# Reordering the decay scan of a two-block model on all engines: level by level instead of unit by unit

## The chip, the cores and the metric

The kernel runs on one core of one Trainium2 chip, in float32. The metric is the device time of one execution in microseconds (us), the median of several runs. The engines are PE (matrix products, with PEld for its weight loads), DVE, ACT, POOL (elementwise work) and SP (starts transfers). Each has its own queue of instructions, worked off in order, and waits on semaphores of the others.

## What is computed

The reference is two transformer blocks of two layers each, 512 tokens by 1024 features. The second block's layers have a mixer of three parts, of which the third is a recurrence with a decay for each key dimension, run forward and backward over the tokens and added (6 heads, keys and values of 64, chunks of 64 tokens; `bt` is the running sum of the log decays):

```
def step(state, inp):
    qt, kt, vt, bt = inp
    diff = bt[:, :, :, None, :] - bt[:, :, None, :, :]
    decay = jnp.where(lower, jnp.exp(jnp.where(lower, diff, 0.0)), 0.0)
    scores = jnp.einsum('bhtk,bhsk,bhtsk->bhts', qt, kt, decay)
    o = (jnp.einsum('bhts,bhsv->bhtv', scores, vt)
         + jnp.einsum('bhtk,bhkv->bhtv', qt * jnp.exp(bt), state))
...
o_r = o_f + o_b
o_r = o_r * lax.rsqrt(jnp.mean(o_r * o_r, axis=-1, keepdims=True) + EPS)
rec = (o_r * jax.nn.silu(g_rec.astype(f32))).astype(h.dtype)
mixed = jnp.concatenate([a, att, rec], axis=-1)
return mixed @ w_out.astype(h.dtype)
```

## The kernel before

The program is a list of phases that every engine walks through. Most of PE's time is in the dense products (line 1320). Each of the two layers of the second block has one phase of kind "scan". It stands between the layer's attention and the rest of the product with `w_out`, and it is all that the change touches.

**Blocks and units.** The six heads lie in three blocks of two (128 partitions). Each block is done in two directions, so a scan has six units, u = 0 to 5: block b = u // 2, direction d = u % 2 (0 forward, 1 backward). Even units are forward, odd ones backward. `blk` and `v` count blocks and levels through both scans.

**A unit's score matrix** of 512 x 512 for each head is built from two kinds of products:
- Pairs. For tiles of 128 tokens that differ, the decay is split at a tile's end: `end_decays` (ACT, exponentials of the sums from `E`) makes factors in `KF` and `QF`, `weigh_ends` (DVE, lines 2580 and 2581, 128x512) multiplies them with keys and queries, `end_queries` (ACT, line 1837) scales three tiles more into `QX`. PE multiplies (line 1215): 20 matmuls in 8 groups forward (the diagonal tiles for both directions are among them, with `KS`, the sum of both directions' keys from POOL, line 2931), 12 in 6 groups backward. Each group goes to one of two PSUM banks, and ACT copies it into `AM` (line 1860).
- Levels. Within the diagonal tiles the decay is split at the middle of sub-blocks of 7 sizes (`LEVELS`: 64, 32, 1, 2, 4, 8, 16). `level_exponents` (DVE, lines 2569 and 2570, 14 instructions of 128x256) makes the differences in `WL`, `level_decays` (ACT, line 1847, one instruction of 128x3584) their exponentials. `weigh_levels` (DVE, line 2592, 7 instructions) multiplies the key half with the keys. `queries` (POOL, line 2910, 28 instructions of 64x128 a unit) multiplies the query half with the queries, into one of eight buffers that lie in spare columns of `X` and `H` (resid and hbuf in the rows). PE multiplies (line 1230, 4 matmuls a level) into one of two PSUM banks. ACT copies the first two levels into `AM` (line 1878), DVE the other five with predicated copies (`merge`, line 2611, two a level).

When both directions of a block are in `AM`, PE multiplies with the values (line 1245, 8 matmuls of 128x512). ACT squares the result (line 1887), PE sums it (`sum_rec`, line 1296), DVE adds epsilon (`begin_finish`, lines 2618 and 2622), POOL takes the root (line 2921), PE spreads it (`spread_rec`, line 1305) and DVE multiplies (`finish`, line 2627).

**Early parts.** The product with `w_out` has 8 output groups. Five eighths of each, whose input is ready before the scan ends, are computed inside the scan: `early` (line 1277, five matmuls of 128x512 for a group from the third on), two PSUM banks in turn; `keep_early` (ACT, line 1899) copies the bank out with a scale, `add_early` (POOL, line 2943) adds it to the residual. `EARLY_AT` says at which unit each group stands.

**Order before.** On PE a unit is: pairs, one early group, 7 levels, and in odd units the values. DVE does, for each unit, the exponents of the next unit, its ends, the five merges of this unit, and the seven weighings of the next. ACT: pair copies, `keep_early`, two level copies, exponentials of the next unit. POOL: all queries of a unit, then an early add, every second time a root. Semaphores tie them: PE's level v waits for `query_ready` (v + 1), for `level_weighed` once a unit, and for `level_taken` (v - 1), which frees the bank.

## Time and profile before

| | us |
|---|---|
| runs | 3520.06, 3520.62, 3513.16 |
| median | 3520.06 |
| the profiled execution | 3523.34 |
| its span | 3521.0 |
| PE busy | 3322.7 (94%) |
| DVE busy | 2146.7 (61%) |
| POOL busy | 1582.4 (45%) |
| ACT busy | 972.7 (28%) |

The rows of the trace are those of the one profiled execution. Its mean granted TensorE clock is 0.969 of 2.4 GHz. The first scan lies from 2073 to 2239 us, the second from 2918 to 3081. A float32 matmul shows as two records, so a level of four matmuls is x8. DVE and ACT start an instruction before the one ahead has ended, so that the distance from start to start is shorter than the duration of one.

### The profile page before, as it was taken

To read this page: it belongs to the slowest core of one execution; us is meant where nothing else is said; L and a number is where in the kernel's file an instruction comes from. 1 tells how busy PE (TensorE), PEld (TensorE's weight loads), DVE (VectorE), ACT (ScalarE), POOL (GpSimd) and SP (SyncE) were. 2 spreads that over 40 slices of the span, in tenths; PEclk is the share of its full clock that TensorE was granted. 3 is DMA by queue.
4 is the path that set the end of the run, shared out by engine and by line. 5 is a ranking of instruction groups with operands and counts; after the bars stand their busy time and mean duration, and the time that the engine had idled before them with its cause. 6 is when DMAs were issued, how large, how long until landed. Compare 5 with 4: busy or idle time off the path is not lost.

```text
span 3521.0 us, 44753 instructions
## 1 busy us (share of the span) xinstructions
PE 3322.7 (94%) x16056; PEld 2551.9 (72%) x16056; DVE 2146.7 (61%) x3556; ACT 972.7 (28%) x2203; POOL 1582.4 (45%) x1534
## 2 busy tenths in 40 slices
PE   8979999999999999999999978899999978899998
PEld 5656555555557967888888746688888865678887
DVE  7577756544544296555646668488764777645554
ACT  2066211001121174211122264322212345332211
POOL 1044322222235224444454458466544547645554
PEclk9999999999999999999999988999999998999999
DMA  7300223333312200344422100244443200022232
GB/s 252 131 3 2 102 79 131 108 114 120 102 56 73 83 1 31 121 161 161 162 91 88 63 12 9 79 145 153 164 142 97 89 28 16 10 88 84 90 90 78
DMA packets 91097, 317.68 MB, mean 90 GB/s; under 512 B 10816, under 2 KB 13152, under 8 KB 90880
## 3 DMA queue, kind: packets, MB, share of 16 engines
q1 hardware_dynamic: 64224, 218.34, 18.9%
q10 hardware_dynamic: 24768, 90.19, 6.9%
q0 software_dynamic: 1888, 6.29, 0.7%
q8 instruction: 132, 2.16, 0.2%
q14 instruction: 85, 0.70, 0.1%
HBM read 312.68 MB, written 2.10 MB: 89 GB/s over the span
## 4 chain that ended last, share of the span: by engine, by line
PE 85%; DVE 9%; ACT 3%; issue 2%; POOL 1%; DMA 0%; DVEq 0%; ACTq 0%; SPq 0%; POOLq 0%
PE ps L1320 64%; PE ps L1322 4%; PE ps L629 3%; PE ps L1277 1%; PE ps L1230 1%; PE ps L985 1%; PE ps L999 1%; PE ps L1021 1%; PE ps L1173 1%; PE ps L1057 1%; PE ps L1215 1%; DVE arena L2611 1%; DVE hbuf L2238 1%; DVE arena L2569 1%; ACT arena L1499 1%
## 5 line engine op out<-in xcount | busy, mean ns | idle before, releaser
L1320 PE MATMUL ps<-arena 128*128 128x256 f32 (+1 forms) x3744 | 951.4, 408 | 4.0 <-DVE arena L2264 3.9
L1320 PEld LDWEIGHTS ps<-arena 128*128 128x128 f32 x3744 | 710.8, 190 | 208.8 <-issue 5.6
L2740 POOL TENSOR_TENSOR arena<-ring,arena 128x512 f32<-128x512 f32 (+1 forms) x140 | 182.6, 1304 | 843.7 <-PE ps L1320 843.7
L1320 PE MATMUL ps<-arena,ring 128*128 128x256 f32 (+1 forms) x2032 | 524.9, 410 | 3.1 <-ACT arena L1668 3.1
L1320 PE MATMUL ps<-hbuf,ring 128*128 128x256 f32 (+1 forms) x1824 | 475.1, 415 | 14.9 <-ACT hbuf L1775 13.4
L1320 PEld LDWEIGHTS ps<-arena,ring 128*128 128x128 f32 x2032 | 385.3, 190 | 119.5 <-ACT arena L1668 5.9
L1320 PEld LDWEIGHTS ps<-hbuf,ring 128*128 128x128 f32 x1824 | 358.3, 197 | 113.7 <-issue 19.1
L2285 DVE TENSOR_TENSOR arena<-ps,arena 128x256 f32<-128x256 f32 (+1 forms) x192 | 86.1, 449 | 362.1 <-PE ps L1320 236.6
L2172 DVE CUSTOM_DVE_ANT_0 aring<-aring,csil,adab 128x1024 f32<-128x1024 f32 x176 | 261.2, 1505 | 1.7
L2290 DVE SCALAR_TENSOR_TENSOR resid<-ps,mod,resid 128x256 f32<-128x256 f32 (+2 forms) x296 | 137.4, 482 | 189.7 <-PE ps L1320 185.1
L2723 POOL TENSOR_TENSOR arena<-ring 128x512 f32<-128x512 f32 (+1 forms) x140 | 179.9, 1285 | 157.2 <-PE ps L1320 149.2
L2290 DVE SCALAR_TENSOR_TENSOR resid<-arena,mod,resid 128x256 f32<-128x256 f32 (+1 forms) x168 | 108.3, 664 | 207.6 <-ACT arena L1668 204.3
L1668 ACT ACTIVATE arena<-ps 128x256 f32<-128x256 f32 (+1 forms) x152 | 62.9, 414 | 610.1 <-PE ps L1320 580.8
L2734 POOL TENSOR_TENSOR arena<-ring 128x512 f32<-128x512 f32 (+1 forms) x140 | 220.8, 1577 | 0.0
L2810 POOL TENSOR_SCALAR arena<-arena,small 128x512 f32<-128x512 f32 (+2 forms) x144 | 98.7, 697 | 239.7 <-DVE small L2053 239.7
L2729 POOL TENSOR_TENSOR arena<-arena,ring 128x512 f32<-128x512 f32 (+1 forms) x140 | 190.4, 1360 | 18.6
L1659 ACT ACTIVATE arena<-ps 128x256 f32<-128x256 f32 (+1 forms) x168 | 68.0, 405 | 469.3 <-PE ps L1320 459.0
L1320 PE MATMUL ps<-hbuf,arena 128*128 128x256 f32 (+1 forms) x672 | 175.8, 404 | 0.0
L2740 POOL TENSOR_TENSOR csil<-ring,junk 128x512 f32<-128x512 f32 x40 | 52.0, 1301 | 227.4 <-PE ps L1320 168.6
L1320 PEld LDWEIGHTS ps<-hbuf,arena 128*128 128x128 f32 x672 | 127.7, 190 | 34.4
L1632 ACT ACTIVATE rstd<-ps 128x256 f32<-128x256 f32 (+1 forms) x180 | 73.6, 409 | 267.9 <-PE ps L1320 250.6
L2379 DVE SCALAR_TENSOR_TENSOR arena<-arena 128x512 f32<-128x512 f32 x88 | 141.8, 1611 | 3.1
(321 smaller groups left out, 5365.5 us busy)
## 6 DMA issues: line engine op xcount, KB each, us to landing
aring<-in_ada ACTq DMA_DIRECT2D x172, 512.0 KB, 4.7
ring<-in_mlp SPq DMA_DIRECT2D x128, 512.0 KB, 3.7
ring<-in_up SPq DMA_DIRECT2D x88, 512.0 KB, 3.3
ring<-in_in SPq DMA_DIRECT2D x56, 512.0 KB, 3.2
ring<-in_down SPq DMA_DIRECT2D x32, 512.0 KB, 3.5
ring<-in_odd_in SPq DMA_DIRECT2D x24, 512.0 KB, 3.2
arena<-in_ada SPq DMA_DIRECT2D x16, 512.0 KB, 13.8
ring<-in_out SPq DMA_DIRECT2D x16, 512.0 KB, 3.2
```

The source lines that it names most:

```text
L629: mm = nc.tensor.matmul(slot[:, lo:hi], ring[:, c % RING, k, :], src[:, kt, lo:hi], start=kt == k0, stop=kt == k0 + nkt - 1)
L1320: return nc.tensor.matmul(ps[:, bank, 0:p.tw], w, x, start=start, stop=stop, skip_group_check=True)
L1322: mm = nc.tensor.matmul(ps[:, bank, t * P:(t + 1) * P], x[:, t * P:(t + 1) * P], w, start=start and t == 0, stop=stop, skip_group_check=True)
L2172: nc.vector.tensor_tensor_reduce(wt, wt, csil[:, 0, :], 1.0, adab[:, layer, nb:nb + 1], ALU.mult, ALU.add, mod[:, layer, nb, 0:1]).then_in ...
L2285: return nc.vector.tensor_tensor(home(p, half, lo, lo + tw), turned_view(p, product), turned_view(p, kept), ALU.add)
L2290: x = nc.vector.scalar_tensor_tensor(out=X[:, blk, a_:b_], in0=src[:, a_ - lo:b_ - lo], scalar=mod[:, layer, p.gate + blk, s_:s_ + 1], in1 ...
L2379: nc.vector.scalar_tensor_tensor(out=v, in0=u[:, 2:S + 2], scalar=CFW[:, blk, 2:3], in1=v, op0=ALU.mult, op1=ALU.add).then_inc(conv_out, 1)
L2723: nc.gpsimd.tensor_tensor(s[0], f1[:, 0:h], f1[:, h:2 * h], ALU.add).then_inc(wsum_ready, 1)
L2729: nc.gpsimd.tensor_tensor(s[1], s[0], f0[:, 0:h], ALU.subtract).then_inc(wsum_ready, 1)
L2734: nc.gpsimd.tensor_tensor(s[2], f0[:, 0:h], f1[:, 0:h], ALU.subtract).then_inc(wsum_ready, 1)
L2740: nc.gpsimd.tensor_tensor(s[3], f0[:, h:2 * h], s[1], ALU.subtract).then_inc(wsum_ready, 1)
L2810: nc.gpsimd.tensor_scalar(v, v, small[:, 12 + i % 4:13 + i % 4], 1.0, ALU.mult, ALU.mult).then_inc(pair_scaled, 1)
```

## The change

The scan is written in another order on every engine. No instruction of the levels and pairs on PE, and none of the exponents, ends, merges and exponentials, is added or dropped.

- DVE: the exponents of unit 1 come before the levels of unit 0, and the ends are weighed two units ahead. Inside a unit each level is weighed and its query made in one go (`weigh_level`, one instruction of 128x256 and two of 64x256), and merges follow two levels behind. The queries have moved here from POOL, where they were 28 instructions a unit.
- PE: the pairs of an odd unit are computed between the levels of the even unit ahead of it, one group behind each level from the second on. The pairs of an even unit follow the values. Early groups 3 to 7 belong to units 0 to 4 and are cut into five single matmuls, one behind each level from the third on; groups 0 to 2 stay ahead of the first pairs. `sum_rec` is ahead of the even units' levels, `spread_rec` behind the second level of the odd units. Each level now waits for its own `level_weighed`.
- ACT: copies one pair group or one level at a time, in PE's order. The exponential of the next unit stands behind the pair copies in even units. At the start it makes the end decays of units 0 and 1 and empties the first early bank before it waits for DVE.
- POOL: keeps the sums of keys, the early adds, the roots and the clearing of the spare columns. Its waits for its own queries are gone.
- The values wait for `so_taken` (the second step of the norm) instead of `syt_taken` (the last).
- In the query buffers each head's part is contiguous, and PE reads its 128 columns as two runs of 64.

```diff
         EARLY_BANK = (5, 7, 5, 7, 5, 7, 5, 7)
-        EARLY_AT = {(0, "ends"): range(0, 3), **{(u, "levels"): range(2 + u, 3 + u) for u in range(1, 6)}}
+        EARLY_FIRST, EARLY_OF = 3, {u: 3 + u for u in range(5)}
         LATE_GROUPS, LATE_K = (0, 1), 2
...
 
             def scan(i):
                 n = scan_phases.index(i)
-                for b in range(3):
+
+                def pair_group(u, hx, j):
+                    b, d = u // 2, u % 2
                     blk = 3 * n + b
...
+                    rows = slice(64 * hx, 64 * hx + 64)
...
+                    pe.wait_ge(unit_ready, 2 * blk + d + 1)
...
+                    if r >= 2:
+
+                        pe.wait_ge(pair_taken, r - 1)
+                    for t in (range(j, 4) if d == 0 else range(j)):
...
+                        mm = nc.tensor.matmul(ps[:, r % 2, t * P:(t + 1) * P], lhs, rhs, start=True, stop=True)
+                    mm.then_inc(pair_ready, 1)
+
+                def level(u, li):
+                    d = u % 2
+                    v = 42 * n + 7 * u + li
...
+                    pe.wait_ge(query_ready, v + 1)
+                    pe.wait_ge(level_weighed, v + 1)
+                    if v % 42 == 0:
+
+                        pe.wait_ge(spare_cleared, 2 * (n + 1))
+                    if v >= 2:
+
+                        pe.wait_ge(level_taken, v - 1)
+                    for t in range(4):
...
+                    mm.then_inc(level_ready, 1)
+
+                def values(b):
+                    blk = 3 * n + b
+
+                    pe.wait_ge(level_taken, 14 * blk + 14)
+                    pe.wait_ge(pair_taken, pair_index(blk, 1, 1, 3) + 1)
+                    if blk >= 1:
+
+                        pe.wait_ge(so_taken, blk)
...
-                        early(i, EARLY_AT.get((2 * b + d, "levels"), ()))
-                        if d == 0 and b >= 1:
-                            sum_rec(blk - 1)
-                        for li in range(7):
...
+                    mm.then_inc(so_ready, 1)
+
+                early(i, range(EARLY_FIRST))
+                for hx in range(2):
+                    for j in range(4):
+                        pair_group(0, hx, j)
+                for u in range(6):
+                    b, d = u // 2, u % 2
+                    if d == 0 and b >= 1:
+                        sum_rec(3 * n + b - 1)
+                    for li in range(7):
+                        level(u, li)
+                        if d == 0 and li >= 1:
+                            pair_group(u + 1, (li - 1) // 3, 1 + (li - 1) % 3)
+                        if li >= 2 and u in EARLY_OF:
+                            k = li - 2
+                            early_part(i, EARLY_OF[u], range(k, k + 1), k == 0, k == EARLY - 1)
+                        if d == 1 and b >= 1 and li == 1:
+                            spread_rec(3 * n + b - 1)
+                    if d == 1:
+                        values(b)
+                        if u < 5:
                             for hx in range(2):
-                                mm = nc.tensor.matmul(ps[64 * hx:64 * hx + 64, SO_BANK, :], VR[:, j, P * b + 64 * hx:P * b + 64 * hx + 64],
-                                                      AM[:, hx, j, :], start=j == 0, stop=j == 3)
-                        mm.then_inc(so_ready, 1)
+                                for j in range(4):
+                                    pair_group(u + 1, hx, j)
                 begin_late(i, LATE_GROUPS[0])
                 sum_rec(3 * n + 2)
                 begin_late(i, LATE_GROUPS[1])
...
                 nc.scalar.activation(roots[:, 0, KT - 1:KT], small[:, 40:41], ACT.Exp)
                 end_decays(0)
+                end_decays(1)
+                keep_early(range(0, 1))
                 end_queries(0)
-                keep_early(EARLY_AT[0, "ends"][0:1])
-                end_decays(1)
-                keep_early(EARLY_AT[0, "ends"][1:2])
                 level_decays(0)
-                keep_early(EARLY_AT[0, "ends"][2:])
+                keep_early(range(1, 2))
+                for hx in range(2):
+                    for j in range(4):
+                        take_pair(0, hx, j)
+                        if (hx, j) == (0, 1):
+                            keep_early(range(2, 3))
+                end_queries(1)
                 for u in range(6):
                     blk, d = 3 * n + u // 2, u % 2
-                    take_pairs(u)
-                    keep_early(EARLY_AT.get((u, "levels"), ()))
-                    take_levels(u)
+                    take_level(u, 0)
+                    take_level(u, 1)
+                    if d == 0:
+                        take_pair(u + 1, 0, 1)
+                        take_pair(u + 1, 0, 2)
+                    end_decays(u + 2)
+                    if d == 0:
+                        take_pair(u + 1, 0, 3)
+                        for j in range(1, 4):
+                            take_pair(u + 1, 1, j)
                     level_decays(u + 1)
-                    end_queries(u + 1)
-                    end_decays(u + 2)
+                    if u in EARLY_OF:
+                        keep_early(range(EARLY_OF[u], EARLY_OF[u] + 1))
+                    end_queries(u + 2)
                     if d == 1:
                         square_values(blk)
+                        if u < 5:
+                            for hx in range(2):
+                                for j in range(4):
+                                    take_pair(u + 1, hx, j)
...
-                def weigh_levels(u):
-                    if u >= 6:
-                        return
+                def weigh_level(u, li):
...
                     dve.wait_ge(level_decay, 6 * n + u + 1)
-                    for li, m in enumerate(LEVELS):
-                        w = WL[:, 7 * (1 - d) + li, :].rearrange("p (g x m) -> p x g m", x=2, m=m)[:, d]
-                        k = KR[:, 3 * d + b, :].rearrange("p (g x m) -> p x g m", x=2, m=m)[:, d]
-                        x = nc.vector.tensor_tensor(w, w, k, ALU.mult)
-                    x.then_inc(level_weighed, 1)
...
+                    both = WL[:, 7 * (1 - d) + li, :].rearrange("p (g x m) -> p x g m", x=2, m=m)
+                    k = KR[:, 3 * d + b, :].rearrange("p (g x m) -> p x g m", x=2, m=m)[:, d]
+                    nc.vector.tensor_tensor(both[:, d], both[:, d], k, ALU.mult).then_inc(level_weighed, 1)
...
+                    if v >= 8:
+
+                        dve.wait_ge(level_ready, v - 7)
+                    w = both[:, 1 - d].rearrange("p (a g) m -> p a g m", a=2)
+                    q = QR[:, b, :].rearrange("p (a g x m) -> p x a g m", a=2, x=2, m=m)[:, 1 - d]
+                    to = level_queries(v).rearrange("p a (h g m) -> p h a g m", h=2, m=m)
+                    for hx in range(2):
+                        rows = slice(64 * hx, 64 * hx + 64)
+                        x = nc.vector.tensor_tensor(to[rows, hx], w[rows], q[rows], ALU.mult)
+                    x.then_inc(query_ready, 1)
+
+                def merge(u, li):
...
+                    dve.wait_ge(pair_taken, pair_index(blk, 0, 1, 3) + 1)
+
+                    dve.wait_ge(level_ready, v + 1)
+
+                    dve.wait_ge(level_taken, v)
...
+                weigh_ends(0)
                 level_exponents(0)
-                weigh_ends(0)
-                weigh_levels(0)
+                weigh_ends(1)
                 for u in range(6):
                     blk, d = 3 * n + u // 2, u % 2
                     level_exponents(u + 1)
-                    weigh_ends(u + 1)
+                    for li in range(7):
+                        weigh_level(u, li)
+                        if li >= 3:
+                            merge(u, li - 1)
+                    merge(u, 6)
+                    if d == 0 and u > 1:
+                        begin_finish(blk - 1)
                     if d == 1 and u > 1:
                         finish(blk - 1)
-                    if d == 0 and u > 1:
-                        begin_finish(blk - 1)
-                    merge(blk, d)
-                    weigh_levels(u + 1)
+                    weigh_ends(u + 2)
                 begin_finish(3 * n + 2)
                 finish(3 * n + 2)
...
-                    def queries(u):
-
...
-                        pool.wait_ge(level_decay, 6 * n + u + 1)
...
-                                rows = slice(64 * hx, 64 * hx + 64)
-                                for half in range(2):
-                                    x = nc.gpsimd.tensor_tensor(dst[rows, half, hx], w[rows, 2 * half:2 * half + 2],
-                                                                q[rows, 2 * half:2 * half + 2], ALU.mult)
-                            x.then_inc(query_ready, 1)
...
-                    def both_keys(b, level):
+                    def both_keys(b):
                         blk = 3 * n + b
-                        if level:
-
-                            pool.wait_ge(query_ready, level)
+                        if b:
+
                             pool.wait_ge(pair_ready, pair_index(blk - 1, 0, 1, 3) + 1)
...
+                    both_keys(0)
+                    def add_early(share):
...
                     for u in range(6):
-                        if u and u % 2 == 0:
-                            both_keys(u // 2, 42 * n + 7 * u)
-                        queries(u)
-                        add_early(EARLY_AT.get((u, "levels"), ()), 42 * n + 7 * u + 7)
+                        if u in (0, 2):
+                            both_keys(u // 2 + 1)
+                        if u in EARLY_OF:
+                            add_early(range(EARLY_OF[u], EARLY_OF[u] + 1))
                         if u >= 2 and u % 2 == 0:
-                            roots(3 * n + u // 2 - 1, 42 * n + 7 * u + 7)
-                    roots(3 * n + 2, 42 * n + 42)
+                            roots(3 * n + u // 2 - 1)
+                    roots(3 * n + 2)
```

PE, first scan, units 0 and 1. Lines 1215, 1230, 1277 and 1245 are pairs, levels, early parts and values. Before:

```order
968 L1215 MATMUL ps<-arena 128x128 x20
969 L1230 MATMUL ps<-resid,arena 128x128 x16
970 L1230 MATMUL ps<-hbuf,arena 128x128 x12
971 L1215 MATMUL ps<-arena 128x128 x12
972 L1277 MATMUL ps<-hbuf,ring 128x512 x5
973 L1230 MATMUL ps<-hbuf,arena 128x128 x4
974 L1230 MATMUL ps<-resid,arena 128x128 x16
975 L1230 MATMUL ps<-hbuf,arena 128x128 x8
976 L1245 MATMUL ps<-arena 64x512 x8
```

After the change, to the middle of unit 0 (lines 1214, 1230 and 1301 are pairs, levels and early parts):

```order
968 L1214 MATMUL ps<-arena 128x128 x20
969 L1230 MATMUL ps<-resid,arena 128x128 x8
970 L1214 MATMUL ps<-arena 128x128
971 L1230 MATMUL ps<-resid,arena 128x128 x4
972 L1214 MATMUL ps<-arena 128x128 x2
973 L1301 MATMUL ps<-hbuf,ring 128x512
974 L1230 MATMUL ps<-resid,arena 128x128 x4
975 L1214 MATMUL ps<-arena 128x128 x3
976 L1301 MATMUL ps<-hbuf,ring 128x512
977 L1230 MATMUL ps<-hbuf,arena 128x128 x4
978 L1214 MATMUL ps<-arena 128x128
979 L1301 MATMUL ps<-hbuf,ring 128x512
```

The 12 pair matmuls of unit 1 and the early group that stood between the two units are now between the levels of unit 0.

DVE, first scan, from the last merges of unit 0 to the first weighings of unit 1. Before, the merges of unit 0 (line 2611) are followed by the weighings of unit 1 (line 2592) at once:

```order
1943 L2611 COPY_PREDICATED arena<-arena,ps 128x4x8x8 x2
1944 L2611 COPY_PREDICATED arena<-arena,ps 128x4x4x16 x2
1945 L2592 TENSOR_TENSOR arena<-arena 128x4x64
1946 L2592 TENSOR_TENSOR arena<-arena 128x8x32
1947 L2592 TENSOR_TENSOR arena<-arena 128x256
1948 L2592 TENSOR_TENSOR arena<-arena 128x128x2
```

After the change (2658 merge, 2618 and 2619 ends, 2607 and 2608 exponents of unit 2; the weighing and the query of a level, 2629 and 2639, come behind the 14 exponents):

```order
1950 L2658 COPY_PREDICATED arena<-arena,ps 128x4x8x8 x2
1951 L2658 COPY_PREDICATED arena<-arena,ps 128x4x4x16 x2
1952 L2618 TENSOR_TENSOR arena<-arena 128x512
1953 L2619 TENSOR_TENSOR arena<-arena 128x512
1954 L2607 TENSOR_TENSOR arena<-aring 128x4x64
1955 L2608 TENSOR_TENSOR arena<-aring 128x4x64
1956 L2607 TENSOR_TENSOR arena<-aring 128x8x32
```

Between the last merge of a unit and the first query of the next there now stand the two instructions on the ends and the 14 exponents of the unit after next.

## Rows read from the trace of the kernel before

**Rows 1.** The page: the chain that ended last, by engine.
```profile
PE 85%; DVE 9%; ACT 3%; issue 2%; POOL 1%; DMA 0%; DVEq 0%; ACTq 0%; SPq 0%; POOLq 0%
```

**Rows 2.** By stretch: length; busy PE, PEld, DVE, ACT, POOL; granted clock; DMA share, GB/s.
```profile
2073.30:2238.70 165.40, 137.94 (x732) 96.45 (x732) 110.79 (x207) 74.76 (x160) 117.08 (x186) 0.89 0.04 13
2917.80:3081.40 163.60, 140.33 (x733) 98.62 (x733) 114.71 (x207) 74.76 (x160) 114.22 (x186) 0.89 0.04 14
2131.00:2136.00 5.00, 4.29 (x24) 4.13 (x24) 3.46 (x8) 3.06 (x11) 4.65 (x9) 0.71 0.02 3
2179.40:2185.70 6.30, 5.46 (x24) 5.20 (x24) 3.59 (x9) 2.43 (x9) 5.89 (x13) 0.54 0.01 4
...
2140.00:2154.00 14.00, 13.85 (x60) 9.38 (x60) 11.15 (x18) 4.64 (x10) 8.99 (x16) 0.76 0.00 0
2189.00:2205.00 16.00, 15.83 (x84) 11.09 (x82) 10.32 (x20) 6.15 (x16) 8.87 (x13) 0.89 0.05 12
2982.00:2996.00 14.00, 13.83 (x56) 8.68 (x54) 10.97 (x19) 4.14 (x10) 8.00 (x14) 0.76 0.00 0
3032.00:3043.00 11.00, 10.83 (x60) 7.62 (x58) 9.86 (x18) 4.52 (x10) 5.96 (x11) 1.00 0.00 0
```

**Rows 3.** PE in order of time, first scan: start, us, line, count, idle before.
```profile
2085.18 6.71 PE L1277 MATMUL ps<-hbuf,ring 128*128 128x512 f32 x10 [4.71 <-ACT junk L1899]
...
2118.06 4.56 PE L1277 MATMUL ps<-hbuf,ring 128*128 128x512 f32 x10
...
2131.06 2.04 PE L1230 MATMUL ps<-resid,arena 128*128 128x128 f32 x8 [4.24 <-DVE arena L2611]
...
2136.20 3.65 PE L1245 MATMUL ps<-arena 128*64 128x512 f32 x16 [0.85 <-DVE arena L2611]
...
2153.80 2.03 PE L1230 MATMUL ps<-hbuf,arena 128*128 128x128 f32 x16
...
2162.95 1.89 PE L1215 MATMUL ps<-arena 64*128 64x128 f32 x14
...
2189.34 5.91 PE L1215 MATMUL ps<-arena 64*128 64x128 f32 x40
...
2202.08 3.09 PE L1230 MATMUL ps<-hbuf,arena 128*128 128x128 f32 x24
...
2210.21 1.09 PE L1305 MATMUL ps<-ident,small 128*64 128x128 f32 x16
...
2228.26 3.65 PE L1245 MATMUL ps<-arena 128*64 128x512 f32 x16 [0.85 <-DVE arena L2611]
...
2238.76 7.13 PE L629 MATMUL ps<-hbuf,ring 128*128 128x512 f32 x16 [0.84 <-DVEq L578]
```

**Rows 4.** DVE in order of time, first scan, columns as in Rows 3.
```profile
2082.76 0.68 DVE L2581 TENSOR_TENSOR arena<-arena 128x512 f32<-128x512 f32 x1
2090.69 2.44 DVE L2592 TENSOR_TENSOR arena<-arena 128x256 f32<-128x256 f32 x7 [7.25 <-ACT arena L1847]
2093.05 0.42 DVE L2569 TENSOR_TENSOR arena<-aring 128x256 f32<-128x256 f32 x1
...
2097.95 1.55 DVE L2580 TENSOR_TENSOR arena<-arena 128x512 f32<-128x512 f32 x1
...
2110.76 0.77 DVE L2611 COPY_PREDICATED arena<-arena,ps 128x256 f32<-128x256 int32 x2 [0.57 <-PE ps L1230]
...
2119.19 0.73 DVE L2569 TENSOR_TENSOR arena<-aring 128x256 f32<-128x256 f32 x1
...
2150.53 0.74 DVE L2618 SCALAR_TENSOR_TENSOR hbuf<-ps,arena 128x512 f32<-128x512 f32 x1
```

**Rows 5.** POOL in the first scan, grouped: one of its two groups of queries.
```profile
L2910 POOL TENSOR_TENSOR resid<-arena 64x128 f32<-64x128 f32 x88 | 48.8, 572 | 6.2 <-issue 3.3
```

**Rows 6.** POOL in order of time, first scan: an early add.
```profile
2092.76 6.19 POOL L2943 TENSOR_TENSOR resid<-resid,junk 128x512 f32<-128x512 f32 x1 [3.77 <-ACT junk L1899]
```

**Rows 7.** ACT in order of time, first scan: the exponential of one unit.
```profile
2106.74 3.19 ACT L1847 ACTIVATE arena<-arena 128x3584 f32<-128x3584 f32 x1
```

153 lines of the change are left out of this document (56 added, 97 removed).

## The prediction

> **What bounds the kernel now.** I read the page first. The chain of work that ended last is 85% PE [rows 1], so time is gained only where PE stands still or runs at the low clock. The change touches only the two scans. The table by stretches gives them: 165.4 and 163.6 us, in which PE is busy 137.9 and 140.3 us, DVE 111 and 115, POOL 117 and 114, and the granted clock is 0.89 in both [rows 2]. So each scan holds about 25 us of PE standing still, and low clock for (1 - 0.89) / 0.5 = 22% of 165 us, 36 us (0.5 is the level of 1.2 GHz, 1.0 that of 2.4). That is the room.
>
> Next the order of time on PE. The reader is to see one wait, 4.24 us for a DVE copy, inside the second unit of a block [rows 3]: DVE works through 14 exponent instructions before it copies level products out. Nothing like it is in the first unit of a block. The DVE rows say why it is slow: the same 128x256 instruction takes 0.42 us at one place and 0.73 at another [rows 4]. POOL is at its 64x128 query instructions at the second place. At the first it has one add under way, which takes 6.19 us, as long as DVE's whole row of instructions [rows 6]. The two hold each other up.
>
> **Names.** A unit u is one direction of one block of two heads; d = u % 2. A scan has units 0 to 5. E is the time at which PE can start level 0 of an even unit. All terms are at the full clock first.
>
> **What the change removes and adds.** POOL loses its query instructions, 168 a scan (28 a unit), 572 ns each in the larger group [rows 5]. DVE gets 14 query instructions a unit, each 64 partitions by 256 elements. The trace has none. The nearest row is its own weighing of 256 elements, 7 in 2.44 us, 0.335 each [rows 4]; the far end is 0.65, for the 0.73 that such an instruction takes beside POOL (0.42 is 0.335 from start to start) [rows 4]. I take 0.335, since POOL's work beside it falls to 14 instructions a scan (three key sums, eight adds, three roots). Weighing and query of one level are then 3 x 0.335 = 1.0 us, a merge (two predicated copies) 0.77 [rows 4].
>
> PE's work is the same. Per level 0.98 us (24 records in 3.09, 8 to a level, less the overlap of the last), a pair matmul 0.27 (14 records, 7 matmuls, in 1.89), an early part 0.88 (five in 4.56, less the overlap: some 4.4 a group), the values 3.6, the 20 pair matmuls of a forward unit 5.9, sum and spread of the norm 0.8 and 1.0 [rows 3]. Only its order changes.
>
> **Even unit (PE sets the pace).** Between levels PE now has pair matmuls and early parts. Up to the end of level 6: 7 levels 6.9, 9 pair matmuls 2.4, four early parts 3.5: 12.8 us. DVE needs 1.77 a level against PE's 2.6 here and is no bound. Behind level 6 PE has 0.8 + 0.9 left.
>
> **Even to odd (DVE sets it).** Behind level 6 on DVE's queue stand: merge 0.9, the first step of the norm 1.0 (0.74 and a small one), weighing the ends 1.3 (two of 0.68), 14 exponents 4.9 (2093.05 to 2097.95), weighing and query of the first level 1.0 [rows 4]: 9.1 us, of which PE fills 1.7. **PE stands still 7.4 us there**, in unit 0 6.4. Before, the queries stood on POOL and this wait was 4.2 us [rows 3]. In unit 4 there are no exponents left to make; the wait is for ACT's exponential of unit 5 (3.19 us [rows 7]), which is now queued behind the last pair copy: the pair 0.8, its copy some 0.7 (an estimate from DVE's 0.74 for a PSUM tile), 3.2 and 1.0 make 5.7 us from level 6.
>
> **Odd unit.** Seven levels, four early parts and the spread: 6.9 + 3.5 + 1.0 = 11.4, then a merge 0.9. DVE's loop of 1.77 fits in PE's 1.9.
>
> **Odd to even (PE sets it).** Values 3.6, pairs 5.9, sum 0.8: 10.3. DVE needs 0.7 + 1.3 + 4.9 + 1.0 = 7.9 in the meantime, so the cover is 2.4 us. In the kernel before, an early group of 4.4 to 6.9 us stood here too; it has gone between the levels.
>
> **The clock.** After a wait of 4 us PE resumed low: 0.71 over 5 us and 0.54 over 6.3, so 2.9 and 5.8 us at the low level; I take 5 us, which costs 2.5 after each of the three waits. After values and forward pairs it went low as well, with PE busy all the time: 0.76 over 14 us twice, 0.89 over 16, 1.00 over 11 [rows 2], so 6.7, 6.7, 3.5 and 0 us, on average 4.2, which costs 2.1 a block. This second kind stands in the even unit after, where PE sets the pace, so I charge it in full.
>
> **The sum for the first scan, by its own clock.** Start: PE ended two early groups at 2080.5 and stood 4.7 us until ACT had emptied a bank [rows 3]. ACT now takes that bank before it waits for DVE, some 3 us earlier. One early group (4.4 to 6.7), the pairs (5.9) and 1 to 2 us for ACT's exponential in the middle of the pair copies: E of unit 0 is 2095.5.
> - Block 0: 12.8 + 8.1 + 10.4 + 0.9 + 10.3 = 42.5, clock 2.5, POOL beside DVE 0.5: E of unit 2 = 2141.0. Before 2153.80 [rows 3].
> - Block 1: 12.8 + 9.1 + 11.4 + 0.9 + 10.3 = 44.5, clock 2.5 + 2.1, POOL 0.9 (an add and the root beside the exponents): E of unit 4 = 2191.0. Before 2202.08 [rows 3].
> - Block 2 to its values: 12.8 + 5.7 + 11.3 (no early parts, so DVE paces: 3 levels and the spread 3.9, then merge, weigh, merge to the end 7.4) = 29.8, clock 4.6: 2225.4. DVE's many satisfied waits, estimated at 0.1 us for some ten levels, add 1: 2226.4. Before 2228.26 [rows 3].
>
> So 12.8 us are ahead at block 1 and 11.1 at block 2, but only 1.8 at the end. The early groups and the pairs have been moved to where they fill waits in blocks 0 and 1, and in block 2 they lie in front of an end that before ran through in 26 us. From the values on nothing changes (2228.26 to 2238.76). The second scan was 1.8 us shorter before and comes out even. In all -1.8 us of 3523.3 of the profiled execution, whose time is 3.3 above the median: **3518 us**. A measurement of this kernel can tell about 0.2%, 7 us, from no change.
>
> **POOL beside DVE.** I charge 1.4 us a scan because the rows show DVE at half its rate beside POOL, not stopped (0.73 against 0.42), and at full rate beside the 6.19 us add [rows 4, 6]. The Trainium skill, in "SBUF — State Buffer", section "SBUF: two separate sides", says that the port pair of these two engines is a lock for a whole instruction and the loser stops. By that rule two adds and a root in the exponents of blocks 0 and 1 would stop DVE for all of their time, twice my charge, and the result would be some 3 us later.
>
> **Bounds of the forecast.** Term by term: the clock after waits 1.5 to 3.1 us each, after the pairs 0 to 3.4, satisfied waits 0 to 3, POOL beside DVE 0 to 3 a scan; the likeliest case alone spans 3508 to 3529.
>
> **Rivals.**
> 1. *The clock holds.* With parts between the levels PE never stops but at three places. If no low stretch follows the pairs (as at 3032 to 3043) and those after waits are as short as the 2.9 us one, each scan gains 2 x 2.1 + 3 x 1.05 = 7.3 more, the two 14.7: 3503 us. With no low clock at all 3494. For it: in the stretch at 3032 the same work ran at 1.00. Against: the wait of 7.4 us is longer than those that brought the clock down.
> 2. *The clock falls more often: slower.* The longer wait and the fine gaps while DVE feeds the odd units give one more low stretch of 6.7 us in each block, at the price of the 14 us row at 0.76 [rows 2]: 3.4 x 3 x 2 = 20 us, 3538 us. It decides for slower from 9 us more of low clock in each scan than I charge (4.5 us each, 9 in all). The Trainium skill, in "TensorE: Matmul & The Clock Gate", section "A second HAM failure mode: psum-queue depth-cycling", describes short idles between groups of matmuls that bring the clock down again and again. The rows speak on both sides: after the same pairs 11 us ran at 1.00 once and 14 at 0.76 twice [rows 2].
> 3. *The query costs more than a weighing: slower.* At 0.65 us each, a level's three instructions take 1.6, DVE's loop 2.4 against PE's 1.9. An odd unit loses 0.6 at its start and 0.5 x 4 in its loop, 2.7; six of them 16 us: 3534 us. It decides from about 0.5 us a query. For: 64 partitions and four-dimensional patterns are untried on DVE. Against: the exponents have patterns as fine and take 0.42.
>
> **How the numbers follow.** Forecast 0.45 (of it 0.14 below 3513, 0.26 within 7 us, 0.05 above 3527), rival 1 0.28, rival 2 0.20, rival 3 0.07. Faster 0.42, same 0.26, slower 0.32. The range 3496 to 3538 leaves out a clock that never falls and the far half of rival 2, no more than 2 in 10.
>
> **What the profile after would show.** Right: PE waits of 6 to 8 us for a DVE instruction of the query line in units 1 and 3 and 4 to 5 in unit 5; no wait of PE for POOL at the levels; exponents on DVE at 0.42 nearly throughout; block starts near 2141 and 2191 if the scan starts at 2073; the scan 163 to 165 us. Wrong: a granted clock of the scan off 0.89 by more than 0.04 (rivals 1 and 2), query rows above 0.5 us (rival 3), PE waits for ACT's pair copies between the levels, or an even unit much longer than 12.8 us.

## The result: slower by 0.74%, and the profile after

The changed kernel takes 3544.13 us (median of 4 runs, 3542.34 to 3549.42), the kernel before beside it 3519.18 us (4 runs, 3513.16 to 3520.62): ratio 1.0074, 95% interval 1.0059 to 1.0089. The forecast was 3518, the range ended at 3538. So the change costs 25 us, and the prediction (2 us faster) was wrong in sign and missed its range by 6 us. Three executions further down took 4399 to 5800 us at a granted clock of 0.555 to 0.742 over the whole program; they are left out of every median.

The profiled execution of after has a span of 3542.5 us, that of before 3521.0. The chain that ended last is made of nearly the same shares as before (POOL 0% for 1%) [rows 1]:

```profile
PE 85%; DVE 9%; ACT 3%; issue 2%; DMA 0%; POOL 0%; DVEq 0%; ACTq 0%; SPq 0%; POOLq 0%
```

The table by stretches (length; busy PE, PEld, DVE, ACT, POOL; granted clock; DMA share, GB/s) of the two scans of after answers to the first two of [rows 2]:

```profile
2066.39:2246.53 180.14, 149.43 (x733) 106.17 (x733) 125.62 (x291) 74.07 (x160) 33.58 (x18) 0.84 0.04 12
2925.13:3103.23 178.10, 145.40 (x733) 103.18 (x733) 125.72 (x291) 74.07 (x160) 33.23 (x18) 0.86 0.04 13
```

The scans grew from 165.4 and 163.6 us to 180.1 and 178.1, by 14.7 and 14.6. POOL's 117 us fell to 34 and DVE's 111 rose to 126, as the change says. The granted clock fell from 0.89 to 0.84 and 0.86. The scans' 29 us are more than the 21.5 of the spans: the first scan of after starts at 2066.39 instead of 2073.35, with nothing changed ahead of it. The trace of before is the odd one here: in the twelve other kernels traced below the first scan starts between 2065.0 and 2070.2. Each trace is one execution, and differs from the median of its kernel by up to 4.4 us.

Where the time of the scans went can be read by cutting them into stretches of 0.5 us. Busy PE times (1 - granted clock) is what the low clock costs; the rest of PE's busy time is what its work would take at the full clock (first and second scan, us):

| | low clock while PE works | PE stands still | PE's work at the full clock | scan |
|---|---|---|---|---|
| before | 14.9, 17.8 | 27.5, 23.2 | 123.0, 122.6 | 165.4, 163.6 |
| after | 24.9, 20.9 | 30.7, 32.7 | 124.5, 124.5 | 180.1, 178.1 |

Of the 29 us that the two scans grew, 13 are low clock, 13 are PE standing still, and 3 are PE's work itself. The low clock is the larger part in the first scan (10.0 of 14.7), the standing still in the second (9.5 of 14.6).

PE in order of time, first scan of after (start, us, line and operation, count, idle before it). Lines: 1214 pairs, 1230 levels, 1245 values, 1301 early parts, 1320 the sum. It answers to [rows 3]:

```profile
2084.52 4.76 PE L1214 MATMUL ps<-arena 64*128 64x128 f32 x20 [0.34 <-ACT arena L1881]
2089.21 4.18 PE L1230 MATMUL ps<-resid,arena 128*128 128x128 f32 x16
...
2094.05 2.07 PE L1230 MATMUL ps<-resid,arena 128*128 128x128 f32 x8
...
2103.04 1.05 PE L1230 MATMUL ps<-hbuf,arena 128*128 128x128 f32 x8
...
2118.01 2.08 PE L1230 MATMUL ps<-hbuf,arena 128*128 128x128 f32 x8 [7.05 <-DVE hbuf L2639]
...
2138.53 4.20 PE L1214 MATMUL ps<-arena 64*128 64x128 f32 x20 [0.23 <-ACT arena L1881]
2142.66 1.86 PE L1320 MATMUL ps<-heads,arena 128*128 128x2 f32 x8
2144.39 3.76 PE L1230 MATMUL ps<-hbuf,arena 128*128 128x128 f32 x16
2148.08 0.79 PE L1214 MATMUL ps<-arena 64*128 64x128 f32 x2
2148.80 1.42 PE L1230 MATMUL ps<-resid,arena 128*128 128x128 f32 x8
2150.15 0.71 PE L1214 MATMUL ps<-arena 64*128 64x128 f32 x4
2150.79 1.12 PE L1301 MATMUL ps<-hbuf,ring 128*128 128x512 f32 x2
...
2170.39 3.41 PE L1230 MATMUL ps<-hbuf,arena 128*128 128x128 f32 x16 [7.92 <-DVE hbuf L2639]
...
2218.97 2.08 PE L1230 MATMUL ps<-resid,arena 128*128 128x128 f32 x8 [4.87 <-DVE resid L2639]
...
2234.45 5.35 PE L1245 MATMUL ps<-arena 128*64 128x512 f32 x16 [0.91 <-DVE arena L2658]
```

Two things are to be seen. The three waits are there, for DVE's query line, and about as long as forecast. And the same eight records of a level take 1.05 us at one place and 2.07 at another, at many places where PE had not waited at all. The stretches in which that is so, first scan (columns as above):

```profile
2084.50:2102.10 17.60, 17.55 (x67) 14.69 (x67) 12.24 (x23) 7.01 (x23) 5.31 (x3) 0.52 0.00 1
2118.00:2122.80 4.80, 4.79 (x25) 4.79 (x26) 3.52 (x9) 1.58 (x6) 0.00 (x0) 0.58 0.00 0
2170.40:2173.80 3.40, 3.40 (x18) 3.28 (x20) 3.30 (x9) 0.65 (x2) 0.71 (x1) 0.58 0.00 0
2219.00:2224.60 5.60, 5.60 (x33) 5.08 (x33) 3.47 (x9) 1.73 (x6) 1.44 (x1) 0.51 0.00 0
2234.40:2239.80 5.40, 5.35 (x17) 1.54 (x17) 0.58 (x1) 0.00 (x0) 0.00 (x0) 0.68 0.00 0
...
2138.50:2150.20 11.70, 11.67 (x55) 10.82 (x55) 5.86 (x13) 3.86 (x12) 1.47 (x1) 0.56 0.00 0
...
2194.60:2202.00 7.40, 7.40 (x37) 6.88 (x37) 2.53 (x8) 2.27 (x8) 0.00 (x0) 0.60 0.01 2
```

In all seven PE is busy from end to end, and the granted clock is 0.51 to 0.68 on average: most of each stretch is at the level of 1.2 GHz. Length times (1 - clock) is what it costs: 8.4 us in unit 0, 2.0 + 1.4 + 2.7 behind the three waits, 5.1 and 3.0 behind the two forward rows of pairs, 1.7 at the last values. That is 24.3 us; the sum of the prediction had 11.7.

DVE, the same scan, from the last exponents of a row on (2607 and 2608 exponents, 2629 weighing, 2639 query, 2658 merge), and POOL's add beside them; they answer to [rows 4, 6]:

```profile
2167.74 0.42 DVE L2608 TENSOR_TENSOR arena<-aring 128x256 f32<-128x256 f32 x1
2168.28 1.28 DVE L2629 TENSOR_TENSOR arena<-arena 128x256 f32<-128x256 f32 x1
2169.49 0.85 DVE L2639 TENSOR_TENSOR hbuf<-arena 64x256 f32<-64x256 f32 x2
2170.37 0.43 DVE L2629 TENSOR_TENSOR arena<-arena 128x256 f32<-128x256 f32 x1
...
2176.00 1.31 DVE L2658 COPY_PREDICATED arena<-arena,ps 128x256 f32<-128x256 int32 x2 [2.00 <-PE ps L1230]
...
2180.70 0.77 DVE L2658 COPY_PREDICATED arena<-arena,ps 128x256 f32<-128x256 int32 x2
```

```profile
2165.75 3.54 POOL L2968 TENSOR_TENSOR resid<-resid,rstd 128x512 f32<-128x512 f32 x1 [21.40 <-ACT rstd L1920]
```

The exponents run at 0.42 us to the last. The add takes 1.26 us at 2217.37, where there is no row of exponents and DVE's two queries take 1.89 us instead of 0.85. Here it takes 3.54, and the weighing behind the row 1.28 instead of 0.42. So POOL got through in the gap behind the exponents, and DVE then waited for it, once in each row.

### The profile page after: what moved, and what is told of

The parts are those of the page before. It is cut to its first block, busy times and chain, and to the rows that moved or that the text cites. A ratio compares the mean times of both kernels' runs of the same rounds, so it can differ in the third digit from the quotient of the medians.

```text
span 3542.5 us, 44643 instructions
## 1 busy us (share of the span) xinstructions
PE 3332.7 (94%) x16056; PEld 2561.8 (72%) x16056; DVE 2178.0 (61%) x3724; ACT 972.4 (27%) x2203; POOL 1420.6 (40%) x1198
## 4 chain that ended last, share of the span: by engine, by line
PE 85%; DVE 9%; ACT 3%; issue 2%; DMA 0%; POOL 0%; DVEq 0%; ACTq 0%; SPq 0%; POOLq 0%
PE ps L1344 63%; PE ps L1346 4%; PE ps L630 3%; PE ps L1230 3%; PE ps L1214 1%; PE ps L986 1%; PE ps L1000 1%; PE ps L1301 1%; PE ps L1174 1%; PE ps L1022 1%; PE ps L1058 1%; ACT hbuf L1799 1%; PE ps L1245 1%; DVE ps L2074 1%; DVE small L2141 1%
## 5 line engine op out<-in xcount | busy, mean ns | idle before, releaser
L1344 PE MATMUL ps<-hbuf,ring 128*128 128x256 f32 (+1 forms) x1824 | 470.2, 412 | 14.7 <-ACT hbuf L1799 13.4
L2790 POOL TENSOR_TENSOR csil<-ring,junk 128x512 f32<-128x512 f32 x40 | 52.2, 1305 | 227.1 <-PE ps L1344 168.3
L2323 DVE TENSOR_TENSOR arena<-ps,rstd 128x256 f32<-128x256 f32 (+1 forms) x144 | 63.6, 442 | 128.9 <-ACT rstd L1692 78.4
```

Source lines behind the costliest of these rows:

```text
L1344: return nc.tensor.matmul(ps[:, bank, 0:p.tw], w, x, start=start, stop=stop, skip_group_check=True)
L2323: return nc.vector.tensor_tensor(home(p, half, lo, lo + tw), turned_view(p, product), turned_view(p, kept), ALU.add)
L2790: nc.gpsimd.tensor_tensor(s[3], f0[:, h:2 * h], s[1], ALU.subtract).then_inc(wsum_ready, 1)
```

## The experiments

Three theories. **A**: the low clock is the bulk of the loss. **B**: the order itself costs, that is PE's groups between the levels and DVE's row of exponents between the units. **C**: the query's place (POOL or DVE) decides. Ratios are against the kernel before, run on the same chip at the same time; its median lay between 3515.2 and 3519.2 us from one chip and session to another, so that ratios compare better than times. Scan lengths (first and second) and clocks are those of the one profiled execution.

### 1. Where the early groups stand

The first kernel is the kernel before with each unit's early group ahead of the unit's pairs:

```diff
+                        early(i, EARLY_AT.get((2 * b + d, "levels"), ()))
                         for hx in range(2):
...
-                        early(i, EARLY_AT.get((2 * b + d, "levels"), ()))
```

> The kernel before with one edit on PE alone: in every unit the early group stands ahead of the pairs instead of behind them. Same instructions, and nothing new to wait for. Theory A (clock): the 64-row pair matmuls let the granted clock fall, and an early group of 128x512 matmuls behind them takes the low stretch and ends it; ahead of the pairs it can't, so low clock falls on the levels. It expects 3523 to 3530 us and a clock of 0.85 to 0.87 over a scan (0.89 in the kernel before). Theory B (queues): the time of the changed kernel comes from DVE's longer queue between even and odd units; the place of early groups in the kernel before is of no weight. It expects 3516 to 3522 us and 0.89.

Measured: 3524.41 us, ratio 1.0022 (1.0012 to 1.0031); scans 170.3 and 167.8. The low stretch behind the forward pairs is now free of any wide matmul, and is low throughout (compare 0.76 and 0.89 in [rows 2]):

```profile
2143.50:2153.80 10.30, 10.30 (x50) 10.05 (x50) 3.53 (x6) 3.76 (x10) 5.15 (x6) 0.51 0.00 0
2194.70:2205.00 10.30, 10.30 (x50) 10.05 (x49) 2.47 (x6) 5.25 (x12) 2.92 (x2) 0.51 0.00 0
```

PE was busy for the whole 10.3 us in both. In the second scan the low stretches behind forward pairs are 10.2 and 7.0 us, where before had 6.8 and none. So in the old order, too, taking the group of 128x512 from behind the pairs lengthens the low stretch. The kernel lost 4 us a scan by the medians (7.4 in all). Only in the first scan is that low clock: by the reckoning of the table above it costs 20.6 us there (14.9 before), but 17.4 in the second (17.8 before), where other low stretches are gone and PE stands still for 4 us more.

The second is the changed kernel with the groups of units 1 and 3 in one piece behind the values and the pairs of the next unit, as before:

```diff
-                        if li >= 2 and u in EARLY_OF:
+                        if li >= 2 and u in EARLY_OF and d == 0:
...
+                        early(i, range(EARLY_OF[u], EARLY_OF[u] + 1))
```

> The changed kernel with the early groups of units 1 and 3 put back whole behind the forward pairs (and their copy on ACT behind the pair copies); odd units lose their slices. Theory A: the clock in the even units 2 and 4 rises from 0.86 and 0.88 to 0.97 or more, which is worth 2 to 4 us at each of the four places. Against it stands that 4.4 us of PE work leave the odd units, where DVE's loop (1.22 for weighing and queries, 0.77 to 1.3 for a merge) is as long as PE's, so that nothing is won there: 17 us in all. Sum for A: 3546 to 3552 us. Theory B expects no change of the clock and the whole 17 us: 3558 to 3563 us.

Measured: 3554.74, ratio 1.0106 (1.0086 to 1.0126); scans 183.0 and 182.9, clock 0.87.

```profile
2142.12 6.45 PE L1302 MATMUL ps<-hbuf,ring 128*128 128x512 f32 x10
2148.41 0.95 PE L1321 MATMUL ps<-heads,arena 128*128 128x2 f32 x8
2149.22 2.03 PE L1230 MATMUL ps<-hbuf,arena 128*128 128x128 f32 x16
```

The group takes the low clock (6.45 instead of 4.4) and the levels behind it are at full clock (2.03 for 16 instead of 3.76). The clock rose by 0.01 to 0.03, and the low clock costs 17.9 us a scan instead of 24.9 and 20.9. Yet the kernel lost 11 us, for PE stands still for 40 us a scan instead of 31 and 33: the odd units, now without a group between their levels, wait for DVE instead (1.26, 1.20 and 0.72 us in unit 1). The result lies between what A and B expected, and says that B has a part.

The third is the changed kernel with the groups of the even units in one piece behind their last level, inside the wait:

```diff
-                        if li >= 2 and u in EARLY_OF:
+                        if li >= 2 and u in EARLY_OF and d == 1:
...
+                    if d == 0:
+                        early(i, range(EARLY_OF[u], EARLY_OF[u] + 1))
```

> The changed kernel with the early groups of the even units 0, 2 and 4 whole behind level 6, inside PE's wait for DVE, instead of between the levels. Theory B: the even unit gets shorter by the four parts ahead of level 6 (3.8 us) down to what DVE's loop allows (some 12 us of 13.7), and the wait of 7 to 8 us shrinks to 3: 1.5 to 3.5 us at each of six places, 3523 to 3535 us. Theory A adds that the 4.4 us of wide matmuls shorten the low stretch at the start of the odd unit: another 1 us at each, and that narrow matmuls alone between the levels may bring the clock down inside the even unit, up to 3 us at each. It expects 3525 to 3545 us with a clock of the even units below 0.86.

Measured: 3529.19, ratio 1.0034 (1.0023 to 1.0045); scans 173.0 and 167.8, at a clock of 0.83 and 0.87. The wait of unit 1 fell from 7.05 to 3.62 us, with 4.4 us of work put into it, and the clock behind it stayed as low as in after:

```profile
2107.20 4.56 PE L1303 MATMUL ps<-hbuf,ring 128*128 128x512 f32 x10
2115.38 2.07 PE L1230 MATMUL ps<-hbuf,arena 128*128 128x128 f32 x8 [3.62 <-DVE hbuf L2641]
```

So 7 to 10 us a scan (7 by the medians) are the place of three early groups: between the levels of a unit that PE paces they lengthen the unit, and the wait behind it, which DVE sets, stays. 3529 us lies in the ranges of both A and B. A also expected that narrow matmuls alone might bring the clock down inside an even unit. They did in unit 0 of the first scan (0.50 over 16 us), but in unit 2, levels and pairs with no early part between them, the clock is full:

```profile
2145.50:2155.40 9.90, 9.10 (x65) 7.65 (x63) 7.90 (x20) 4.46 (x16) 0.00 (x0) 1.00 0.01 2
```

### 2. Dummy matmuls that keep PE from standing still

The changed kernel with 7, 8 and 5 wide matmuls (the identity by the normalized tile, 128x512, into a free bank, never read) in the three waits:

```diff
+                    if d == 0:
+                        pe.wait_ge(early_taken, KT * n + EARLY_OF[u])
+                        for _ in range((7, 8, 5)[b]):
+                            nc.tensor.matmul(ps[:, EARLY_BANK[(EARLY_OF[u] + 1) % 8], :], ident[:, :], H[:, 0, 0:S], start=True, stop=True)
```

> The changed kernel with 7, 8 and 5 matmuls of 128x512 that nobody reads (identity times a tile, into the free early bank) in PE's wait between the even and the odd unit of blocks 0, 1 and 2. They take 6.2, 7.0 and 4.4 us of waits of 7.1, 7.9 and 4.9. Theory A: the low stretches at the start of the odd units vanish (PE was low there for 4.2, 3.0 and 5.6 us): 6.4 us less a scan, 3531 us. Theory B: the wait itself costs, the clock does not: 3542 to 3547 us.

Measured: 3529.87, ratio 1.0032 (1.0019 to 1.0045); scans 173.2 and 171.1, clock 0.90 and 0.92.

```profile
2111.42 6.17 PE L1269 MATMUL ps<-hbuf,ident 128*128 128x512 f32 x14
2118.64 1.16 PE L1230 MATMUL ps<-hbuf,arena 128*128 128x128 f32 x8 [1.05 <-DVE hbuf L2643]
```

Nothing but useless work was added, and the kernel is 14 us faster than after. The low clock costs 16.8 and 12.6 us in the scans, 8 less in each than in after. The levels behind the wait run at the full clock (1.16 for 8 instead of 2.08), and the pairs that follow later are better too (3.43 instead of 4.20). A is shown for this part of the loss.

Both together (the groups in the wait, then 4, 5 and 2 dummies):

> The changed kernel with the even units' early groups whole in PE's wait for DVE (as in the run of that name) and the rest of the wait filled with 4, 5 and 2 matmuls of 128x512 that nobody reads. Theory A: low clock at the start of the odd units goes: 4 to 6 us less a scan than the 3529 us without the filling, 3517 to 3521 us. Theory B: 3527 to 3531 us.

Measured: 3520.27, ratio 1.0013 (1.0004 to 1.0023); both scans 164.3 at a clock of 0.92. The two repairs mostly add up (by the ratios 14 us for the groups and 15 for the dummies alone, 21 for both), and lead back to the scan length of the kernel before, not below it.

### 3. Where the queries are made

Half of the changed kernel's queries on POOL (of each level one 64x256 on DVE and one on POOL), and all of them on POOL, in both ahead of POOL's other work of the same unit. Of the first, DVE's line and POOL's loop:

```diff
-                    for hx in range(2):
+                    for hx in range(1):
...
+                            for hx in range(1, 2):
+                                rows = slice(64 * hx, 64 * hx + 64)
+                                x = nc.gpsimd.tensor_tensor(dst[rows, hx], w[rows], q[rows], ALU.mult)
```

> The changed kernel with the second head's query of each level (one instruction of 64x256) back on POOL; PE waits for both halves. DVE's level falls from 1.22 to 0.8 us. Theory B (DVE's queue sets the time): 0.4 us less before the first level of each odd unit, and the waits between the levels of unit 5 (1.6 + 1.2 + 0.7 us) and 3 go: 4 to 5 us less a scan, 3534 to 3537 us, if POOL beside DVE costs nothing. Theory C (POOL and DVE hold each other up): DVE's exponents and ends, 4.9 + 1.3 us in the wait between even and odd units, go up again to as much as 0.67 each where POOL's queries fall beside them, 3 to 4 us at each of two or three places: 3544 to 3552 us.

> The changed kernel with all queries back on POOL, in its own form (two instructions of 64x256 a level, not four of 64x128); the order of PE, ACT and DVE stays. It is the reordering without the move of the queries. Theory B: DVE's level costs 0.35, the odd units are paced by PE alone, and the first level of an odd unit comes 0.9 us earlier: 5 to 6 us less a scan, 3532 to 3535 us. Theory C: POOL needs 14 x 0.8 = 11 us a unit and DVE's exponents slow down beside it, so the wait between even and odd units grows by 2 to 4 us: 3545 to 3560 us. Theory A (clock) alone: no change, 3544 us, with 50 us or more of low clock a scan.

Measured: half 3544.47, ratio 1.0083 (1.0068 to 1.0098), scans 178.0 and 178.2; all 3561.41, ratio 1.0133 (1.0117 to 1.015), scans 186.2 and 186.3. Taking 42 instructions a scan off DVE gains nothing, taking all 84 loses 17 us (21 by the ratios). The rows of DVE and POOL, grouped (count, busy us, mean ns), of the kernel with all on POOL:

```profile
L2629 DVE TENSOR_TENSOR arena<-arena 128x256 f32<-128x256 f32 x42 | 25.9, 650 | 3.4 <-ACT arena L1871 2.8
L2607 DVE TENSOR_TENSOR arena<-aring 128x256 f32<-128x256 f32 x42 | 25.8, 614 | 0.0
...
L2948 POOL TENSOR_TENSOR resid<-arena 64x256 f32<-64x256 f32 x44 | 36.0, 817 | 2.9
```

POOL takes 0.82 us for each of the two queries of a level, while DVE's exponents beside it take 0.61 instead of 0.42. PE's waits between the units become 7.73 and 10.26 us, for POOL. Part of them is POOL's own queue: behind ACT's exponential (to 2109.85) it first does the early add of the unit before (2.67 us from 2110.57), then the first query; in block 1 the root stands there as well (1.74 us).

Then the other way round: the kernel before with POOL's queries in the changed kernel's wide form (two of 64x256 a level instead of four of 64x128), and the kernel before with the wide queries on DVE, behind each weighing, nothing else changed:

```diff
                         nc.vector.tensor_tensor(w, w, k, ALU.mult).then_inc(level_weighed, 1)
+                        for hx in range(2):
+                            rows = slice(64 * hx, 64 * hx + 64)
+                            x = nc.vector.tensor_tensor(to[rows, hx], w[rows], q[rows], ALU.mult)
+                        x.then_inc(query_ready, 1)
```

> The kernel before with only the new layout of the query buffers, and with it 14 POOL queries of 64x256 a unit instead of 28 of 64x128. If an instruction's fixed part on POOL weighs, a unit's queries fall from 15 us to some 11, PE's waits for POOL in unit 0 (3.3 + 2.6 us) shrink and DVE is slowed for a shorter time: 3505 to 3512 us. If POOL's time goes by elements alone: 3515 to 3519 us. The new layout itself, 128 columns read as two runs of 64, is not expected to cost anything on PE (1.05 us a level in both kernels at the full clock).

> The kernel before in its own order on all engines; only the query instructions are moved from POOL to DVE, in the changed kernel's form (two of 64x256 behind each weighing), with the changed kernel's layout of the query buffers. This is one half of the change alone. The order of everything else is that of the kernel before. Theory A (the two halves are not additive: the move was worth 17 us in the changed order because there the levels wait for each query; in the old order the queries were hidden but for unit 0, and DVE now has 8.5 us of weighing and queries ahead of 5.9 us of exponents and the copies out): the wait inside the odd units grows from 4.2 to about 6 us, unit 0 wins 3, exponents are at 0.42 us: scans of 164 to 168 us, 3515 to 3524 us. Theory B (the move is worth the same 17 us in either order, since it is POOL's hold on DVE that costs, and the whole loss of the changed kernel is in its order): 3498 to 3503 us, scans of 156 to 158 us.

Measured: wide on POOL 3522.28, ratio 1.002 (1.0011 to 1.003), scans 168.3 and 167.3; on DVE 3525.24, ratio 1.0019 (1.0011 to 1.0028), scans 167.1 and 166.9. Both are misses upward (the second by 1 us). The first one is the more telling. POOL is busy 68 us instead of 89 with its queries, and yet PE's wait inside unit 1 grows from 4.24 to 7.03 us. DVE's rows of that kernel say why:

```profile
2109.04 6.41 DVE L2593 TENSOR_TENSOR arena<-arena 128x256 f32<-128x256 f32 x7
2115.37 0.94 DVE L2570 TENSOR_TENSOR arena<-aring 128x256 f32<-128x256 f32 x1
...
2122.53 0.41 DVE L2571 TENSOR_TENSOR arena<-aring 128x256 f32<-128x256 f32 x1
```

While POOL's queries of 0.82 us run, each DVE instruction starts 0.86 to 0.90 us after the last, in the kernel before 0.58 to 0.65 (0.73 from start to end [rows 4]) beside POOL's 0.57 [rows 5]; without POOL 0.335. In both kernels the starts say that the two take turns, one instruction each (POOL's eight queries from 2108.78 stand 0.91 us apart, DVE's seven weighings beside them 0.90), so that DVE's pace follows the length of POOL's instruction. Longer instructions on POOL save POOL time and cost DVE time.

So moving the queries to DVE gains 17 to 21 us in the new order, against wide queries on POOL. In the old order it gains nothing against the same wide queries (1.0019 and 1.0020) and loses 7 us against the narrow ones. C is no cause by itself. Narrow queries on POOL were not run in the new order, so how much of the 17 us is the engine, how much the width and how much the queue is not shown.

### 4. The kernel before with dummies: faster than both

Four wide dummies in the wait of 4.2 us of units 1 and 3 of the kernel before:

```diff
+                            if d == 1 and b < 2 and li == 4:
+                                pe.wait_ge(early_taken, KT * n + 2 * b + 3)
+                                for _ in range(4):
+                                    nc.tensor.matmul(ps[:, EARLY_BANK[2 * b + 2], :], ident[:, :], H[:, 0, 0:S], start=True, stop=True)
```

> The kernel before, plus four wide dummy matmuls (identity by the normalized tile, 128x512, some 3.6 us) in the wait of 4.2 us in units 1 and 3 of each scan, into a bank that nobody uses then; their result is not read. Theory A (the low clock behind the wait is on the path): the records behind the wait run at the full clock, the one of 2.04 us for 8 at 1.05, the next at 2.0, the early group of 6.9 behind the pairs shorter: 2 to 4 us less a scan, 3508 to 3512 us. Theory B (DVE's copies set the pace there, and the clock falls anyway behind the forward pairs): within 2 us a scan of no change, 3514 to 3519 us.

Measured: 3511.19, ratio 0.9979 (0.997 to 0.9989); both scans 160.5. PE in order of time, unit 1, and below it the stretch from the dummies on (columns as above):

```profile
2117.84 3.60 PE L1229 MATMUL ps<-hbuf,ident 128*128 128x512 f32 x8
2121.27 1.05 PE L1234 MATMUL ps<-resid,arena 128*128 128x128 f32 x8
...
2117.80:2128.80 11.00, 10.09 (x50) 5.34 (x49) 9.89 (x18) 5.80 (x11) 10.36 (x18) 1.00 0.01 1
```

The level behind the wait takes 1.05 instead of 2.04 us [rows 3], and the granted clock is 1.00 up to the values (0.71 in [rows 2]). The kernel is 7 us below before, and some 33 below after.

The same in the kernel of part 3 with DVE's queries in the old order (six dummies), and, in the version just shown, eight more at the start of the scan and ahead of unit 0's levels:

> The first kernel of this call (queries on DVE in the old order) with six such dummy matmuls in the longer wait of units 1 and 3. If the wait there is about 6 us (theory A of that run) and the clock behind it is on the path, it is 4 to 8 us below that kernel: 3509 to 3518 us. If the clock falls anyway, or DVE sets the pace behind the wait, it is within 3 us of it.

> The kernel before with the four dummy matmuls in units 1 and 3 (the version of 3511 us), and besides five of them in the wait of 4.7 us behind the first two early groups of a scan and three in front of the first level of unit 0. Theory A (low clock behind those two waits is on the path as well): the third early group takes 4.6 us instead of 6.0 to 6.7, the pairs 5.9 instead of 6.5 to 7.0, and block 0 starts no later: 1 to 3 us less a scan than in the version with four dummies (160.5 us), 3504 to 3510 us. Theory B (at the start of a scan ACT's exponentials, DVE's exponents and POOL's queries set the pace, and PE's clock costs nothing there): 160 to 162 us a scan, 3510 to 3514 us.

Measured: 3518.66, ratio 0.9996 (0.9987 to 1.0005), scans 165.5 and 165.6, which is 7 us below the same kernel without dummies, as expected; and 3509.94, ratio 0.9981 (0.9972 to 0.999), scans 161.0 twice at a clock of 0.93. More dummies at the scan's start raise the clock and gain nothing. PE's first level begins 5 us later than with four dummies (29.6 us after the scan's start instead of 24.7), and yet the pairs of unit 1 begin at 37.8 instead of 38.7: between the two it is not PE that sets the pace.

## Why the prediction was wrong

**What held.** The waits: 7.05 us (6.4 predicted) into unit 1, 7.92 (7.4) into unit 3, 4.87 (4 to 5) into unit 5. No wait of PE for POOL at the levels; exponents at 0.42; the query at 0.42 for 64x256, so rival 3's 0.65 was not the way, though its sign was. POOL beside DVE was a small thing as priced, by another mechanism: the "half rate" that I read from 0.73 against 0.42 [rows 4] was turns taken with POOL instructions of 0.57. The Trainium skill says in "SBUF — State Buffer", section "SBUF: two separate sides", that the port pair is a lock for a whole instruction. The traces agree: 1.28 us instead of 0.42 behind rows of exponents, and the turns of 0.86 to 0.90 us when POOL's instructions were made longer.

**The step that failed: the clock.** The first scan took 180.1 us where the sum gave 163.6, 16.5 more. The term for the clock was 11.7 a scan and measured 24.3 (in the second scan 20.9, with 14.5 us more than the sum in all). By place:

| place, first scan | priced, us | measured, us |
|---|---|---|
| unit 0, pairs and first levels | 0 | 8.4 |
| behind the three waits | 7.5 | 6.1 |
| behind forward pairs, blocks 1 and 2 | 4.2 | 8.1 |
| last values | 0 | 1.7 |

The price per wait was about right. Wrong was to carry over the old low stretch behind the pairs as an average of 2.1 us, though the change takes away what stood there: an early group of 128x512 that PE ran before the levels. In the old order that group carried part of the low stretch and levels ran at full clock behind it. In the new one pairs, sum and levels follow each other, all narrow, and the low stretch is longer: 10.2 and 7.0 us in each scan. It isn't the early parts that end it: the clock is back before the first of them (at 2148.80 a level takes 1.42 us, the early part follows at 2150.79), and in unit 0 the first early part itself ran low (2.07 us). The first experiment shows the longer stretch in the old order alone (10.3 us at 0.51), the second shows it undone (7.0 and 3.5 us with the group back behind the pairs). And unit 0 was summed at the full clock altogether: 12.8 us to the end of its last level in the sum, 19.8 measured (2089.21 to 2109.04). Why it ran low for 17 us there isn't shown: in the second scan, with the same instructions, it was 10. Some 2 of its 8.4 us lay in the pairs, beside DVE (in the second scan PE waited 2.02 us there), so that about 10.5 of the 16.5 us are the clock.

**The rest, some 6 us a scan,** is several terms that were each a little small. A level's weighing and query take 1.22 us, not 1.0: of 0.335 for each only the weighing is right, two queries of half the partitions take 0.84 together. The merges of the levels with sub-blocks of 1 and 2 take 1.31 us each, not 0.77; the same durations stood in the trace of before (1.32 us at 2107.33, 1.31 at 2108.88), and POOL is no cause, for it is idle beside 2176.00. On PE an early part between levels takes 0.96 instead of 0.88 and a pair group 0.41 to 0.86 instead of 0.27 to 0.80, so an even unit at the full clock is 13.7 us, not 12.8. The weighing of 1.28 adds 0.9 to the waits into units 1 and 3, two queries of 1.89 beside an add 1.0 to that into unit 5. For the 1 us of DVE's satisfied waits no run shows a figure; what is measured is a level's 1.22 us from start to start, waits included.

**The rivals.** Rival 2, at 3538 and with a chance of 0.20, named the right quantity, more low clock, but not its place: it put one more low stretch a block down to the longer wait and to gaps in the odd units, and behind the waits the clock cost less than charged (6.1 us against 7.5). What grew is behind the pairs. It was given too small a chance: of the four stretches after forward pairs in [rows 2] only one was free of low clock, and all four had the wide group. Its condition, "from 9 us more of low clock in each scan than I charge", was met: the low stretches' 24.3 us against 11.7 are 25 us more at half speed.

**What the reorder is worth at like clocks.** With dummies in both (clocks 0.90 to 0.92) the new order with the early groups in the wait takes 164.3 us a scan, the old one 160.5. With the queries on DVE in both, 164.3 and 165.5. That is no gain of the order: the low clock costs 12.6 us in the one and 15.4 in the other, and by the ratios the new order is 6 us slower in all (1.0013 against 0.9996). So the new order itself is worth nothing that the runs show. DVE's queries cost 5 us a scan in the old one (165.5 against 160.5; 3 by the ratios), and the early groups between the levels 7 to 9 (171.1 and 173.2 against 164.3; 3 by the ratios). The longer even unit and the wait behind it were both in the sum, and about right; not seen was that they need not be paid together, since the groups fit into the wait.

**What stays open.** Why the clock falls behind forward pairs at some times and not at others, with the same instructions, and how long it stays low: the runs show where it falls and what shortens it, no rule. No run moved DVE's row of exponents alone, so its share of the 13 us that PE stood still longer isn't shown. And why the first scan starts at 2065 in one run and at 2073 in another.
